# A fused transformer-like layer on one core: three modulation rows moved forward in a hand-written order, and four small edits around the router

## The chip, the cores and the metric

The kernel runs on one core of one Trainium2 chip. The metric is the device time of one execution in microseconds (us), the median of several. The engines are TensorE (PE, matrix products), VectorE (DVE), ScalarE (ACT), GpSimd (POOL) and SyncE (SP, which here only starts transfers). They run side by side, each its own list of instructions in order, and meet at semaphores: an engine stops at a wait until another has counted the semaphore up.

## The reference, cut to what matters

One residual layer for 256 tokens (`S`) of width 2048 (`D`), all in float32:

```
ada = silu(c) @ w_ada + b_ada                  # w_ada: 2048 x (6 x 2048)
sh_m, sc_m, gt_m, sh_f, sc_f, gt_f = split(ada, 6)
h  = rms_norm(x, g_pre_mix) * (1 + sc_m) + sh_m
y  = token_mixer(h)      # h @ w_in; attention heads || gated linear attention; @ w_out
x1 = x + gt_m * rms_norm(y, g_post_mix)
h  = rms_norm(x1, g_pre_ffn) * (1 + sc_f) + sh_f
y  = hier_moe(h)         # top-1 group of 8 experts, top-2 experts inside it, 32 experts in all
x  = x1 + gt_f * rms_norm(y, g_post_ffn)
```

with `rms_norm(x, g) = x * rsqrt(mean(x*x) + 1e-6) * g`. An expert is `(silu(t @ w1) * (t @ w3)) @ w2`, its three matrices 4 MB each.

## The kernel before, in words

**Stages.** The first 230 us build the first two modulation vectors and a first part of the input projection. Then a list called `SCHED`, made by `schedule()` and walked by every engine in the same order, holds the rest of the mixer: 28 slots, each one part of a product with `w_in` on PE (L832; 16 matmul records, some 7 us), and beside it pieces of attention, of the linear attention and of the modulation. After the slots come the output units: products of the mixer's output with `w_out` (two units of two token halves, then the last two quarters of the columns as seven half-size products called `prod` 0 to 6). Then x1, the router, and the experts, one loop pass per tile of 32 token rows.

**Modulation rows.** The four remaining modulation vectors (m = 2 to 5) are matrix-vector products done by DVE: 64 row blocks of `w_ada`, 1 MB each, are loaded by SP and multiplied and added into an accumulator (`accumulate`, L1320 for the first block of a vector, L1322 for the others). They are numbered 1 to 64 here; blocks 33 to 48 are vector 4, blocks 49 to 64 vector 5. The table `ADA_IN` (L78) says how many of them stand in each slot, 28 slots and the four output units; within a slot they stand ahead of the slot's pieces of linear attention. Four buffers hold them, so SP starts the load of a block when the block four earlier has been used (L573 and L574). `loads()` also derives SP's own order from the same table: the blocks are queued in between the loads of the weight units; those of the `w_out` units 8 and 9 (4 MB each, L568) come where the slots 23 and 27 end, four blocks ahead of DVE's use.

**Linear attention at the end of the slots.** PE makes `kv` (L890), DVE turns it into states (L1481, L1483), PE reads them out (`glao`, L900), ACT squares, POOL takes the roots, and DVE multiplies the result by its gate (`gmul`, L1492; (0,0) in slot 26, (1,0) and (0,1) in slot 27, (1,1) behind). Then `glaT` (L910) on PE transposes the first token half; it waits for `gla_sb` to reach 3, that is for three of the four `gmul`, and it stands in PE's list between the last slot product and the first output unit (L923).

**Queues.** SP's transfers and ACT's go through one DMA queue each. ACT starts the row gain `g1b` and the load of unit 10 (L1870) after the second output unit, and half units of 2 MB (L1859, L1872) later.

**Around x1.** For each token half t, ACT squares the quarters of y with a sum (`square_of`), DVE adds the four sums (`total_of`), POOL makes the inverse root in two steps (`rms`: L1976 scale and add, L1979 power), DVE forms x1 (L1510). PE transposes x1 and makes the logits, DVE routes (L1523 to L1576), PE picks the first tile's rows (`pick_rows`, L1014), DVE copies them (L1596), PE transposes them (L1026), DVE scales and shifts (L1599, L1602), and the first expert's products begin (L1064).

**Expert loads.** Five weight buffers of 4 MB. The halves of the first five matrices are started by SP as the `prod` products free their space. All further ones are started as PE passes points of the expert loop, the first of them (L629) behind the first quarter of the first product of expert 0's last tile (`a_half`).

Of the kernel before, what the change touches and what calls it, by code (L numbers as in the profile page):

```python
# [26 lines left out]
D = 2048  # L27
S = 256
P = 128
TT = S // P  # L30
# [10 lines left out]
EPS = 1e-6  # L41
# [10 lines left out]
C_ID, C_LT, C_SUF, C_ONE, C_IOTA, C_NH, C_HALF, C_FOLD, C_FLIP, C_PAIR, C_BKT = 0, 128, 256, 384, 512, 544, 548, 550, 582, 710, 774  # L52
# [22 lines left out]
FILLS = HELD + SLOTS // 2 - 2 * len(BLOCK_UNITS)  # L75
ATT_FROM = 4
MOD_AFTER = {2: 7, 3: 16}
ADA_IN = [1, 1, 1, 1, 1, 1, 1, 1, 2, 2, 2, 2, 0, 3, 3, 3, 2, 2, 2, 1, 1, 3, 3, 2, 2, 2, 2, 1, 4, 4, 4, 4]  # L78
ADA_SLOT = [s for s, n in enumerate(ADA_IN) for _ in range(n)]


# [145 lines left out]
def build(nc, a, out):  # L227
    f32, i32, u32 = mybir.dt.float32, mybir.dt.int32, mybir.dt.uint32
    ALU, ACT, AX = mybir.AluOpType, mybir.ActivationFunctionType, mybir.AxisListType
    SCHED = schedule()  # L230
    ctx = ExitStack()
    with ctx:
# [14 lines left out]
        cst = sb("cst", [P, C_KEEP])  # L247
# [3 lines left out]
        gains = sb("gains", [P, 4, KD])  # L251
        bada = sb("bada", [P, 6, KD])
        mod = sb("mod", [P, 6, KD])
# [3 lines left out]
        st = sb("st", [P, 84])  # L257
# [14 lines left out]
        y, x1T = view(s3, 0, TT, D), view(s4, 0, KD, S)  # L272
# [3 lines left out]
        junk = wk[:, 3584:4096]  # L276
# [21 lines left out]
        xp = wk[:, 2560:3072]  # L298
        wr, wrf = view(wrs, 0, KD, RT_N), wrs
        hit, gated, pick = view(wrf, 0, 2 * TT, ROWS), view(wrf, 128, 2 * TT, ROWS), view(wrf, 256, TT, ROWS)  # L300
# [5 lines left out]
        def rows(t):  # L306

            return resid[:, TT - 1 - t, :].rearrange("p (k q) -> p k q", k=KD)
# [55 lines left out]
        def bank(b, *dims):  # L364
            if not dims:
                return ps[:, b, :]
            return ps[:, b, 0:dims[0] * dims[1]].rearrange("p (n c) -> p n c", n=dims[0])
# [49 lines left out]
        def ada_quarter(n):  # L417
# [36 lines left out]
        g_sb, g_out, x1_row, g_in, xre_in = sem("g_sb"), sem("g_out"), sem("x1_row"), sem("g_in"), sem("xre_in")  # L454
        y_tot, y_sum, y_rs, x1_sb, x1_sq, x1_rs = sem("y_tot"), sem("y_sum"), sem("y_rs"), sem("x1_sb"), sem("x1_sq"), sem("x1_rs")
        x1T_ps, x1T_dve, x1T_act, logT_sb, shs_sb, shs_ps, wr_sb = sem("x1T_ps"), sem("x1T_dve"), sem("x1T_act"), sem("logT_sb"), sem("shs_sb"), sem("shs_ps"), sem("wr_sb")
        pick_sb, pick_c, rows_ps, rows_sb = sem("pick_sb"), sem("pick_c"), sem("rows_ps"), sem("rows_sb")
        gate_c, gated_sb, spread_ps, spread_sb, part_ps, ysum_sb = (
            sem("gate_c"), sem("gated_sb"), sem("spread_ps"), sem("spread_sb"), sem("part_ps"), sem("ysum_sb"))
        log_ps, g_max, e_max, r_exp2, m_sb, rank_ps, route_sb = (  # L460
            sem("log_ps"), sem("g_max"), sem("e_max"), sem("r_exp2"), sem("m_sb"), sem("rank_ps"),
            sem("route_sb"))
# [208 lines left out]
        def _(pe):  # L671
# [3 lines left out]
            for t in range(TT):  # L675
                pe.wait_ge(diag_sb, t + 1)
                for j in range(4):
                    if t and j == 3:
                        pe.wait_ge(xT_sb, 1)
                    for k in range(4):  # L680
                        last = nc.tensor.matmul(bank((4 * t + j) % 7, 4, P)[:, k, :], resid[:, t, P * (4 * j + k):P * (4 * j + k) + P], diag[:, t, :], start=(k == 0), stop=(k == 3))
# [43 lines left out]
            for j in range(len(STAGES)):  # L725
                pe.wait_ge(early_w_in[j % 3], 16 * sum(slab_count(i) for i in range(j % 3, j + 1, 3)))
                for n, u in enumerate(TURN):
# [6 lines left out]
                    last = early_unit(j, u)  # L734
# [9 lines left out]
            for item in SCHED:  # L744
                kind = item[0]
                if kind == "mod":
                    m = item[1]
# [8 lines left out]
                elif kind == "alpha":  # L756

                    if item[1] == 0:
# [3 lines left out]
                        for k in range(KD):  # L762
                            last = nc.tensor.matmul(bank(5)[32 * (k % 4):32 * (k % 4) + 32, 0:S], wzb[:, k, :], hT[:, k, :], start=(k < 4), stop=(k >= KD - 4))
# [114 lines left out]
                elif kind == "kv":  # L878
                    t = item[1]
# [130 lines left out]
            def pick_rows():  # L1010

                for t2 in range(TT):
                    for g in range(4):
                        last = nc.tensor.matmul(bank(0)[32 * g:32 * g + 32, :], pick[:, t2, :], rows(t2)[:, g:KD:4, :], start=(t2 == 0), stop=(t2 == TT - 1))  # L1014
                last.then_inc(rows_ps, 1)
# [12 lines left out]

            pe.wait_ge(x1_row, TT)
            pe.wait_ge(pick_sb, 1)  # L1030
            pick_rows()
            pe.wait_ge(route_sb, 1)
            first_hi = pe.value_load(cums[0:1, 1:2], min_val=1, max_val=MAX_TILES)
            for h in range(2):
# [127 lines left out]
        def _(dve):  # L1162
# [161 lines left out]
            def take_mod(m):  # L1324
                dve.wait_ge(mod_ps, m - 1)
                V.tensor_tensor(mod[:, m, :], mod_bank(m)[:, 16 * m:16 * m + 16], bada[:, m, :], ALU.add).then_inc(mod_sb, 1)
                dve.wait_ge(mod_sb, m - 1)
                if m == 4:
                    V.scalar_tensor_tensor(out=mod[:, m, :], in0=mod[:, m, :], scalar=1.0, in1=gains[:, 2, :], op0=ALU.add, op1=ALU.mult).then_inc(scale_sb, 1)
                    dve.wait_ge(scale_sb, 1)  # L1330
                if m in (2, 5):
                    V.tensor_tensor(mod[:, m, :], mod[:, m, :], gains[:, 1 if m == 2 else 3, :], ALU.mult).then_inc(g_sb, 1)

            def gain_y(u, t):

                if u < 2:
                    dve.wait_ge(proj_sb, FILLS + 2 * u + t + 1)
                else:
                    dve.wait_ge(y_sum, {(2, 0): 5, (3, 0): 6, (3, 1): 7, (2, 1): 8}[u, t])
                dve.wait_ge(g_in, 16)  # L1340
                c = slice(512 * u, 512 * u + 512)
                link(V.tensor_tensor(y[:, t, c], y[:, t, c], g1b[:, c], ALU.mult))

            def total_of(t):
                dve.wait_ge(y_sum, 6 + 2 * t)
                V.tensor_reduce(st[:, 56 + t:57 + t], st[:, 48 + 4 * t:52 + 4 * t], axis=AX.X, op=ALU.add).then_inc(y_tot, 1)

            def sum_of(out_, in0, in1, n, op=ALU.add):

                V.tensor_tensor(out_, in0, in1, op).then_inc(mix_sb, 1)  # L1350
                dve.wait_ge(mix_sb, n)

            def y_at(t, u):
                return y[:, t, 512 * u:512 * u + 512]
# [141 lines left out]
            for t in range(TT):  # L1496
                if t:
                    dve.wait_ge(proj_ps, FILLS + 10)
                    sum_of(y_at(1, 2), y_at(1, 3), bank(4), 13)
                    sum_of(y_at(1, 3), y_at(1, 2), bank(3), 14)  # L1500
                    dve.wait_ge(proj_ps, FILLS + 11)
                    sum_of(y_at(1, 2), y_at(1, 2), bank(1), 15)
                    gain_y(3, 1)
                else:
                    gain_y(2, 0)
                total_of(t)
                gain_y(2 if t else 3, t)
                dve.wait_ge(y_rs, t + 1)
                dve.wait_ge(xre_in, 32)
                V.scalar_tensor_tensor(out=x_again(t), in0=y[:, t, :], scalar=st[:, 58 + t:59 + t], in1=x_again(t), op0=ALU.mult, op1=ALU.add).then_inc(x1_sb, 1)  # L1510
# [81 lines left out]

                return mod[:, m, 8 * h:8 * h + 8].unsqueeze(2).to_broadcast((P, 8, ROWS))

            def copy_rows(h):
                V.tensor_copy(xp[:, S * h:S * h + S], bank(0)[:, S * h:S * h + S]).then_inc(rows_sb, 1)  # L1596

            def scaled(h):
                return V.tensor_tensor(xe[:, 8 * h:8 * h + 8, :], bank(3 + h, 8, ROWS), by_column(4, h), ALU.mult)  # L1599
# [8 lines left out]
            link(V.tensor_copy(gates[:, :, :], R("w")))  # L1608
            dve.nop(nofuse=True).then_inc(route_sb, 1)
            V.memset(spread, 0.0).then_inc(spread_sb, 1)  # L1610
            dve.wait_ge(rows_ps, 1)
            for h in range(2):
                copy_rows(h)
            for h in range(2):
                dve.wait_ge(xe_ps, h + 1)
                scaled(h).then_inc(xe_t, 1)
# [77 lines left out]
        def _(act):  # L1694
# [49 lines left out]
            def squares(t):  # L1744

                act.wait_ge(x1_sb, t + 1)
                A(acc[:, :] if t else resid[:, 1, :], x_again(t), ACT.Square, accum_out=st[:, 60 + t:61 + t]).then_inc(x1_sq, 1)
                act.wait_ge(x1_sq, t + 1)

            def order_rows(t):  # L1750

                if t:
                    act.wait_ge(x1_row, t)
                A(rows(t), x_again(t).rearrange("p (q k) -> p k q", k=KD), ACT.Copy).then_inc(x1_row, 1)
# [123 lines left out]

            def square_of(t, u, mixed_n, n):

                act.wait_ge(y_sum, n - 1)
                act.wait_ge(mix_sb, mixed_n)
                A(junk, y[:, t, 512 * u:512 * u + 512], ACT.Square, accum_out=st[:, 48 + 4 * t + u:49 + 4 * t + u]).then_inc(y_sum, 1)

            square_of(0, 2, 6, 5)
            square_of(0, 3, 12, 6)
            squares(0)
            order_rows(0)
            square_of(1, 3, 14, 7)
            square_of(1, 2, 15, 8)  # L1890

            for t in range(TT):
# [71 lines left out]
        def _(pool):  # L1964
            n_c = [0]

            def link(ins):

                ins.then_inc(pool_c, 1)
                n_c[0] += 1  # L1970
                pool.wait_ge(pool_c, n_c[0])

            def rms(src, dst, width):

                n = src.shape[1]
                nc.gpsimd.tensor_scalar(dst, src, 1.0 / width, EPS, ALU.mult, ALU.add).then_inc(pool_c, 1)  # L1976
                n_c[0] += 1
                pool.wait_ge(pool_c, n_c[0])
                return nc.gpsimd.tensor_tensor(dst, dst, cst[:, C_NH:C_NH + n], ALU.pow)  # L1979
# [53 lines left out]
            pool.memset(ye, 0.0).then_inc(ye_sb, 1)  # L2033
            for t in range(TT):
                pool.wait_ge(y_tot, t + 1)
                rms(st[:, 56 + t:57 + t], st[:, 58 + t:59 + t], D).then_inc(y_rs, 1)
                pool.wait_ge(x1_sq, t + 1)
                rms(st[:, 60 + t:61 + t], st[:, 62 + t:63 + t], D).then_inc(x1_rs, 1)
            pool.wait_ge(g_sb, 2)
            pool.dma_start(gdram[1, :, :], mod[:, 5, :]).then_inc(g_out, 16)  # L2040

            pool.wait_ge(x1_sq, TT)
            pool.memset(ysum[0], 0.0).then_inc(ysum_sb, 1)
            pool.wait_ge(mod_ps, 4)
# [26 lines left out]
```

## Time and profile before

| | us |
|---|---|
| median of 3 runs | 1452.66 |
| lowest, highest | 1451.88, 1452.72 |
| the profiled execution, its own time | 1452.2 |
| span of its profile | 1450.3 |

| engine | busy in the span |
|---|---|
| PE | 84% |
| DVE | 54% |
| ACT | 15% |
| POOL | 4% |

Transfers move 583.52 MB, at 402 GB/s over the span. The chain of waits that ended last is 42% DMA and 33% PE. Such a share is a mean over stages with different limits; what one stage is limited by is read from that stage's rows.

### The profile page before, as it was taken

How to read it: one execution, taken by the hardware profiler on the slowest of the kernel's cores; microseconds unless marked ns; L12 is line 12 of the kernel's file. 1: busy time of each engine (PE TensorE's matmuls, PEld its weight loads, DVE VectorE, ACT ScalarE, POOL GpSimd, SP SyncE). 2: the span in 40 equal slices, each digit the busy share in tenths (PEclk: the TensorE clock that was granted, in tenths of full speed). 3: DMA queues.
4: the chain of work that ended last, by engine and by line, in shares of the span. 5: the costliest groups of instructions: out<-in, count | busy, mean ns of one | idle time of the engine just before them, and what ended most of it. 6: DMA issues, size and time to landing. Idle time of an engine off the chain costs nothing.

```text
span 1450.3 us, 18992 instructions
## 1 busy us (share of the span) xinstructions
PE 1221.5 (84%) x7437; PEld 573.8 (40%) x7438; DVE 780.4 (54%) x1106; ACT 210.4 (15%) x489; POOL 53.6 (4%) x76
## 2 busy tenths in 40 slices
PE   4899999999999989877776667767776679999967
PEld 3678788644444443222232222222222223333322
DVE  5777379897888765433343234323332335555525
ACT  3011131223111041000010001000000001111103
POOL 1000300020000020000000000000000000000020
PEclk9999999999999999888788789888888889999989
DMA  9999977999999899999999999999999999999996
GB/s 354 389 389 377 311 294 293 389 374 382 411 411 405 316 390 423 430 431 431 432 432 433 430 432 431 433 431 432 433 431 431 431 433 433 431 432 431 431 427 263
DMA packets 81653, 583.52 MB, mean 402 GB/s; under 512 B 5376, under 2 KB 30256, under 8 KB 56912
## 3 DMA queue, kind: packets, MB, share of 16 engines
q1 hardware_dynamic: 74256, 564.41, 94.4%
q10 hardware_dynamic: 5808, 14.85, 2.7%
q0 software_dynamic: 1552, 3.75, 0.9%
q8 instruction: 25, 0.41, 0.1%
q14 instruction: 12, 0.10, 0.0%
HBM read 579.30 MB, written 3.69 MB: 402 GB/s over the span
## 4 chain that ended last, share of the span: by engine, by line
DMA 42%; PE 33%; DVE 3%; issue 1%; ACT 1%; POOL 0%; SPq 0%; ACTq 0%; DVEq 0%
DMA stream<-in_w 41%; PE ps L1064 9%; PE ps L832 6%; PE ps L1120 4%; PE ps L1071 3%; PE ps L1020 2%; PE ps L923 2%; PE ps L1014 2%; DVE stream L1350 1%; PE ps L928 1%; PE ps L932 1%; DMA stream<-in_w_out 1%; PE ps L1026 0%; PE ps L890 0%; PE ps L900 0%
## 5 line engine op out<-in xcount | busy, mean ns | idle before, releaser
L1064 PE MATMUL ps<-stream,wk 128*32 128x512 f32 x2304 | 330.0, 711 | 178.8 <-DMA stream<-in_w 178.1
L1589 DVE TENSOR_TENSOR acc<-ps,acc 128x2048 f32<-128x2048 f32 x37 | 84.8, 2291 | 359.2 <-PE ps L1020 359.2
L1064 PEld LDWEIGHTS ps<-stream,wk 128*32 128x32 f32 x2304 | 74.7, 125 | 417.3 <-issue 329.9
L1120 PE MATMUL ps<-stream,cst 128*32 128x512 f32 x1152 | 131.5, 595 | 7.8 <-DMA stream<-in_w 7.8
L717 PE MATMUL ps<-stream 128*128 128x256 f32 x512 | 117.0, 388 | 6.3 <-DVE stream L1196 2.1
L832 PE MATMUL ps<-stream 128*128 128x512 f32 x256 | 112.7, 593 | 0.0
L717 PEld LDWEIGHTS ps<-stream 128*128 128x128 f32 x512 | 99.1, 194 | 26.9 <-issue 7.8
L1071 PEld LDWEIGHTS ps<-cst,wk 128*128 128x128 f32 x576 | 77.3, 209 | 69.7 <-issue 69.7
L1020 PE MATMUL ps<-wk,cst 32*128 32x512 f32 x592 | 92.1, 694 | 0.8 <-ACT wk L1929 0.8
L1210 DVE SCALAR_TENSOR_TENSOR wk<-stream,cc,wk 128x768 f32<-128x768 f32 (+1 forms) x90 | 83.5, 928 | 11.2 <-DMA stream<-in_w_ada 8.6
L1071 PE MATMUL ps<-cst,wk 128*128 128x32 f32 x576 | 85.5, 295 | 0.0
L1589 DVE TENSOR_TENSOR wk<-ps,wk 128x2048 f32<-128x2048 f32 x36 | 82.2, 2282 | 1.6 <-PE ps L1020 1.6
L1322 DVE SCALAR_TENSOR_TENSOR acc<-stream,cc,acc 128x2048 f32<-128x2048 f32 x30 | 70.4, 2348 | 10.0 <-DMA stream<-in_w_ada 8.9
L1637 DVE TENSOR_SCALAR cst<-cst 128x128 f32<-128x128 f32 x36 | 8.2, 228 | 116.3 <-ACT cst L1923 116.3
L1014 PE MATMUL ps<-resid,wrs 128*32 128x512 f32 x592 | 70.2, 592 | 0.2 <-DVE wrs L1576 0.2
L832 PEld LDWEIGHTS ps<-stream 128*128 128x128 f32 x256 | 47.5, 190 | 55.1 <-issue 55.1
L1120 PEld LDWEIGHTS ps<-stream,cst 128*32 128x32 f32 x1152 | 35.9, 109 | 77.7 <-issue 62.2
L1921 ACT ACTIVATE wk<-ps 128x512 f32<-128x512 f32 x36 | 21.5, 597 | 268.8 <-PE ps L1064 268.8
L965 PE MATMUL ps<-stream 128*128 128x512 f32 x112 | 48.6, 594 | 2.0 <-DMA stream<-in_w_out 2.0
L784 PE MATMUL ps<-stream 128*128 128x256 f32 x224 | 49.9, 381 | 0.3 <-PE ps L717 0.3
L1596 DVE COPY wk<-ps 128x256 f32<-128x256 f32 x74 | 27.9, 419 | 36.2 <-PE ps L1014 36.2
L784 PEld LDWEIGHTS ps<-stream 128*128 128x128 f32 x224 | 42.1, 190 | 7.1 <-issue 1.6
(291 smaller groups left out, 1151.9 us busy)
## 6 DMA issues: line engine op xcount, KB each, us to landing
stream<-in_w SPq DMA_DIRECT2D x87, 4096.0 KB, 41.8
stream<-in_w_ada SPq DMA_DIRECT2D x64, 1024.0 KB, 7.7
stream<-in_w SPq DMA_DIRECT2D x16, 2048.0 KB, 11.5
stream<-in_w_in SPq DMA_DIRECT2D x7, 4096.0 KB, 15.5
stream<-in_w_ada SPq DMA_DIRECT2D x64, 384.0 KB, 9.8
stream<-in_w_ada SPq DMA_DIRECT2D x16, 512.0 KB, 9.7
stream<-in_w_in SPq DMA_DIRECT2D x4, 2048.0 KB, 13.4
stream<-in_w_out SPq DMA_DIRECT2D x2, 4096.0 KB, 17.3
```

What stands on the lines that cost most here:

```text
L717: last = nc.tensor.matmul(bank(u if held else HELD, 2, S)[:, part, :], home(k, k + 1)[:, 0, 256 * u + P * part:256 * u + P * part + P], hT ...
L784: last = nc.tensor.matmul(block_bank(b, n), left[:, k, :], right[:, k, :], start=(k == 0), stop=(k == 7))
L832: last = nc.tensor.matmul(bank(fill % 2), hT[:, k, P * half:P * half + P], w[:, k, :], start=(k == 0), stop=(k == KD - 1))
L965: last = nc.tensor.matmul(bank(b), left[:, k, :], right[:, k, :], start=(k == 0), stop=(k == 7))
L1014: last = nc.tensor.matmul(bank(0)[32 * g:32 * g + 32, :], pick[:, t2, :], rows(t2)[:, g:KD:4, :], start=(t2 == 0), stop=(t2 == TT - 1))
L1020: last = nc.tensor.matmul(ps[:, b0 + g, :], spread[32 * g:32 * g + 32, t2, :], ye[32 * g:32 * g + 32, :], start=not onto, stop=True)
L1064: last = nc.tensor.matmul(bank(1 + m)[32 * g:32 * g + 32, :], xe[:, k + g, :], w13[m][:, k + g, :], start=(k == 0), stop=(k == KD - 4))
L1071: last = nc.tensor.matmul(bank(1 + m, 4, ROWS)[:, c, :], ab[m][:, P * c:P * c + P], cst[:, C_FOLD:C_FOLD + ROWS], start=True, stop=True)
L1120: last = nc.tensor.matmul(bank(2)[32 * g:32 * g + 32, :], hid[:, k, :], w2v[:, k, 512 * g:512 * g + 512], start=(k == 0), stop=(k == 3))
L1210: ins = V.scalar_tensor_tensor(out=out_, in0=w, scalar=cc[:, 2, k:k + 1], in1=out_, op0=ALU.mult, op1=ALU.add)
L1322: V.scalar_tensor_tensor(out=acc_m, in0=w, scalar=col, in1=acc_m, op0=ALU.mult, op1=ALU.add).then_inc(ada_done, 1)
L1589: V.tensor_tensor(y4, ps[:, b0:b0 + 4, :], y4, ALU.add).then_inc(ysum_sb, 1)
```

## The change

1. `ADA_IN`: the entries of slots 23 and 24 go from 2 to 3, those of slots 25 and 26 stay 2, slot 27 goes from 1 to 2, and the first three output units get 3 instead of 4. So 51 blocks instead of 48 stand ahead of the output units.
2. x1's root: DVE's `total_of` now adds a sum of three made earlier (`first_three`), the fourth and `D * EPS`, so that POOL takes the power alone. The factor `sqrt(D)` goes into the gain of vector 2. ACT squares quarter 3 of the second half before it orders the first half's rows, and writes the sums in another order.
3. The first picking is done in two halves of 256 columns into two PSUM banks, each with its own semaphore, and each copy waits for its half alone.
4. POOL's clearings of the two expert sums (2048 columns each) wait for `route_sb`, which follows the router's counts.

```diff
-ADA_IN = [1, 1, 1, 1, 1, 1, 1, 1, 2, 2, 2, 2, 0, 3, 3, 3, 2, 2, 2, 1, 1, 3, 3, 2, 2, 2, 2, 1, 4, 4, 4, 4]
+ADA_IN = [1, 1, 1, 1, 1, 1, 1, 1, 2, 2, 2, 2, 0, 3, 3, 3, 2, 2, 2, 1, 1, 3, 3, 3, 3, 2, 2, 2, 3, 3, 3, 4]
...
             pe.wait_ge(pick_sb, 1)
-            pick_rows()
+            for n in range(2):
+                for t2 in range(TT):
+                    for g in range(4):
+                        last = nc.tensor.matmul(bank(5 * n)[32 * g:32 * g + 32, S * n:S * n + S], pick[:, t2, :], rows(t2)[:, g + 8 * n:8 * n + 8:4, :], start=(t2 == 0), stop=(t2 == TT - 1))
+                last.then_inc(rows_ps if n else log_ps, 1)
...
             def total_of(t):
                 dve.wait_ge(y_sum, 6 + 2 * t)
-                V.tensor_reduce(st[:, 56 + t:57 + t], st[:, 48 + 4 * t:52 + 4 * t], axis=AX.X, op=ALU.add).then_inc(y_tot, 1)
+                V.tensor_scalar(st[:, 56 + t:57 + t], st[:, 51 + 4 * t:52 + 4 * t], st[:, 4 + t:5 + t], D * EPS, ALU.add, ALU.add).then_inc(y_tot, 1)
+
+            def first_three(t):
+                dve.wait_ge(y_sum, 5 + 2 * t)
+                link(V.tensor_reduce(st[:, 4 + t:5 + t], st[:, 48 + 4 * t:51 + 4 * t], axis=AX.X, op=ALU.add))
...
                     sum_of(y_at(1, 3), y_at(1, 2), bank(3), 14)
+                    first_three(1)
+                    gain_y(3, 1)
                     dve.wait_ge(proj_ps, FILLS + 11)
                     sum_of(y_at(1, 2), y_at(1, 2), bank(1), 15)
-                    gain_y(3, 1)
                 else:
                     gain_y(2, 0)
+                    first_three(0)
                 total_of(t)
...
-            dve.wait_ge(rows_ps, 1)
             for h in range(2):
-                copy_rows(h)
+                dve.wait_ge(*((rows_ps, 1) if h else (log_ps, 3)))
+                copy_rows(h, 5 * h)
...
             squares(0)
+            square_of(1, 3, 14, 7)
             order_rows(0)
-            square_of(1, 3, 14, 7)
             square_of(1, 2, 15, 8)
...
                 pool.wait_ge(y_tot, t + 1)
-                rms(st[:, 56 + t:57 + t], st[:, 58 + t:59 + t], D).then_inc(y_rs, 1)
+                nc.gpsimd.tensor_tensor(st[:, 58 + t:59 + t], st[:, 56 + t:57 + t], cst[:, C_NH:C_NH + 1], ALU.pow).then_inc(y_rs, 1)
...
+            pool.wait_ge(route_sb, 1)
             pool.wait_ge(x1_sq, TT)
             pool.memset(ysum[0], 0.0).then_inc(ysum_sb, 1)
             pool.wait_ge(mod_ps, 4)
             pool.memset(ysum[1], 0.0).then_inc(ysum_sb, 1)
-            pool.wait_ge(route_sb, 1)
```

DVE's list from slot 21 to the first output unit, before. `acc` and `wk` are the accumulators of vectors 4 and 5, `resid` holds the states, `stream` behind L1492 the gated result:

```order
L1322 SCALAR_TENSOR_TENSOR acc<-stream,cc,acc 128x2048 x8
L1481 COPY resid<-ps 128x256 x4
L1483 SCALAR_TENSOR_TENSOR resid<-resid,st,ps 128x256 x4
L1322 SCALAR_TENSOR_TENSOR acc<-stream,cc,acc 128x2048 x2
L1483 SCALAR_TENSOR_TENSOR resid<-resid,st,ps 128x256 x8
L1322 SCALAR_TENSOR_TENSOR acc<-stream,cc,acc 128x2048 x4
L1492 SCALAR_TENSOR_TENSOR stream<-ps,st,stream 128x256 x2
L1322 SCALAR_TENSOR_TENSOR acc<-stream,cc,acc 128x2048
L1492 SCALAR_TENSOR_TENSOR stream<-ps,st,stream 128x256 x6
L1320 TENSOR_SCALAR wk<-stream,cc 128x2048
L1322 SCALAR_TENSOR_TENSOR wk<-stream,cc,wk 128x2048 x3
```

The same piece of DVE's list now (its line numbers are those of the changed file: L1326 is the old L1322, L1324 the old L1320, L1500 the old L1492):

```order
L1326 SCALAR_TENSOR_TENSOR acc<-stream,cc,acc 128x2048 x9
L1489 COPY resid<-ps 128x256 x4
L1491 SCALAR_TENSOR_TENSOR resid<-resid,st,ps 128x256 x4
L1326 SCALAR_TENSOR_TENSOR acc<-stream,cc,acc 128x2048 x3
L1491 SCALAR_TENSOR_TENSOR resid<-resid,st,ps 128x256 x8
L1326 SCALAR_TENSOR_TENSOR acc<-stream,cc,acc 128x2048 x3
L1324 TENSOR_SCALAR wk<-stream,cc 128x2048
L1500 SCALAR_TENSOR_TENSOR stream<-ps,st,stream 128x256 x2
L1326 SCALAR_TENSOR_TENSOR wk<-stream,cc,wk 128x2048 x2
L1500 SCALAR_TENSOR_TENSOR stream<-ps,st,stream 128x256 x6
L1326 SCALAR_TENSOR_TENSOR wk<-stream,cc,wk 128x2048 x3
```

One more block now stands ahead of the first states, two ahead of the last states, and three ahead of the six gate multiplications at the end, of which the first four are those that `glaT` waits for.

SP's list around the two loads of `w_out` units, before:

```order
L565 DMA stream<-in_w_in 128x16x512
L574 DMA stream<-in_w_ada 128x2048 x9
L568 DMA stream<-in_w_out 128x16x512
L574 DMA stream<-in_w_ada 128x2048 x7
L568 DMA stream<-in_w_out 128x16x512
L574 DMA stream<-in_w_ada 128x2048 x12
```

and now:

```order
L565 DMA stream<-in_w_in 128x16x512
L574 DMA stream<-in_w_ada 128x2048 x10
L568 DMA stream<-in_w_out 128x16x512
L574 DMA stream<-in_w_ada 128x2048 x9
L568 DMA stream<-in_w_out 128x16x512
L574 DMA stream<-in_w_ada 128x2048 x9
```

One block is queued ahead of unit 8 that stood behind it, and three ahead of unit 9.

## Rows read from the trace of the kernel before

**Rows 1.** Windows: us, busy of each engine, TensorE clock, DMA share, GB/s.

```profile
core 0: us, PE busy (x) PEld busy (x) DVE busy (x) ACT busy (x) POOL busy (x), PEclk, DMA share, GB/s
600.00:1400.00 800.00, 624.55 (x4732) 221.24 (x4728) 317.16 (x565) 77.58 (x158) 0.00 (x0) 0.88 1.00 432
...
540.00:544.00 4.00, 3.75 (x36) 1.15 (x40) 2.41 (x9) 0.04 (x1) 0.00 (x0) 1.00 0.54 164
```

**Rows 2.** Timeline of PE: start, us, line, shapes, count [idle before it, ended by].

```profile
381.58 1.95 PE L900 MATMUL ps<-resid,stream 128*64 128x256 f32 x16
...
394.33 14.00 PE L832 MATMUL ps<-stream 128*128 128x512 f32 x32
408.37 1.09 PE L910 MATMUL ps<-cst,stream 128*128 128x128 f32 x8
...
467.84 34.60 PE L965 MATMUL ps<-stream 128*128 128x512 f32 x80 [2.03 <-DMA stream<-in_w_out]
```

**Rows 3.** Timeline of DVE, slot 21 to the output units.

```profile
358.12 19.56 DVE L1322 SCALAR_TENSOR_TENSOR acc<-stream,cc,acc 128x2048 f32<-128x2048 f32 x8
377.60 1.41 DVE L1481 COPY resid<-ps 128x256 f32<-128x256 f32 x4
379.04 1.66 DVE L1483 SCALAR_TENSOR_TENSOR resid<-resid,st,ps 128x256 f32<-128x256 f32 x4
...
385.50 3.35 DVE L1483 SCALAR_TENSOR_TENSOR resid<-resid,st,ps 128x256 f32<-128x256 f32 x8
...
398.87 4.83 DVE L1322 SCALAR_TENSOR_TENSOR acc<-stream,cc,acc 128x2048 f32<-128x2048 f32 x2 [5.30 <-DMA stream<-in_w_ada]
...
406.67 1.65 DVE L1492 SCALAR_TENSOR_TENSOR stream<-ps,st,stream 128x256 f32<-128x256 f32 x4
...
427.17 4.80 DVE L1322 SCALAR_TENSOR_TENSOR wk<-stream,cc,wk 128x2048 f32<-128x2048 f32 x2 [2.79 <-DMA stream<-in_w_ada]
```

**Rows 4.** Windows, as Rows 1: two stretches before the output units.

```profile
378.00:398.87 20.87, 20.87 (x84) 10.02 (x83) 15.20 (x21) 3.52 (x17) 2.88 (x5) 1.00 1.03 404
398.87:411.30 12.43, 12.39 (x36) 5.73 (x35) 11.45 (x13) 2.17 (x5) 0.00 (x0) 1.00 1.02 422
```

**Rows 5.** The DMA issue at 408.36: timeline, then issues (KB, us to landing).

```profile
408.36 0.38 SPq L568 DMA_DIRECT2D stream<-in_w_out  x1
...
stream<-in_w_out SPq DMA_DIRECT2D x1, 4096.0 KB, 16.2
```

**Rows 6.** Idle PE and the clock behind it: timeline, then windows as Rows 1.

```profile
594.96 5.34 PE L1064 MATMUL ps<-stream,wk 128*32 128x512 f32 x32 [2.62 <-DMA stream<-in_w]
605.12 2.71 PE L1064 MATMUL ps<-stream,wk 128*32 128x512 f32 x16 [3.75 <-DMA stream<-in_w]
...
596.00:600.00 4.00, 4.00 (x28) 0.87 (x17) 0.00 (x0) 0.00 (x0) 0.00 (x0) 0.59 0.98 422
604.00:612.00 8.00, 6.88 (x36) 2.92 (x40) 1.71 (x4) 0.28 (x1) 0.00 (x0) 0.63 1.01 434
```

**Rows 7.** Timeline around the second half's root: DVE and POOL.

```profile
518.39 0.69 DVE L1342 TENSOR_TENSOR stream<-stream,acc 128x512 f32<-128x512 f32 x1
...
513.14 0.19 POOL L1976 TENSOR_SCALAR st<-st 128x1 f32<-128x1 f32 x1 [4.57 <-ACT resid L1747]
...
518.53 0.60 POOL L1976 TENSOR_SCALAR st<-st 128x1 f32<-128x1 f32 x1 [4.56 <-DVE st L1346]
519.21 0.54 POOL L1979 TENSOR_TENSOR st<-st,cst 128x1 f32<-128x1 f32 x1
```

**Rows 8.** Timeline of DVE in the router, beside POOL's second clearing.

```profile
529.21 0.49 DVE L1531 TENSOR_SCALAR wk<-wk 128x2 f32<-128x2 f32 x1
```

**Rows 9.** Timeline of PE: a logit product, then the first picking and transposing.

```profile
518.81 2.03 PE L985 MATMUL ps<-stream,wrs 128*64 128x128 f32 x32 [0.44 <-ACT stream L1895]
...
536.29 1.92 PE L1014 MATMUL ps<-resid,wrs 128*32 128x512 f32 x16 [0.24 <-DVE wrs L1576]
538.75 0.77 PE L1026 MATMUL ps<-cst,wk 128*128 128x128 f32 x4 [0.54 <-DVE wk L1596]
```

More of the change, by code:

```diff
@@ L1331, in take_mod @@
                 if m in (2, 5):
-                    V.tensor_tensor(mod[:, m, :], mod[:, m, :], gains[:, 1 if m == 2 else 3, :], ALU.mult).then_inc(g_sb, 1)
+                    V.scalar_tensor_tensor(out=mod[:, m, :], in0=mod[:, m, :], scalar=math.sqrt(D) if m == 2 else 1.0, in1=gains[:, 1 if m == 2 else 3, :], op0=ALU.mult, op1=ALU.mult).then_inc(g_sb, 1)
             def gain_y(u, t):
@@ L1593, in by_column, with copy_rows @@
                 return mod[:, m, 8 * h:8 * h + 8].unsqueeze(2).to_broadcast((P, 8, ROWS))
-            def copy_rows(h):
-                V.tensor_copy(xp[:, S * h:S * h + S], bank(0)[:, S * h:S * h + S]).then_inc(rows_sb, 1)
+            def copy_rows(h, b=0):
+                V.tensor_copy(xp[:, S * h:S * h + S], bank(b)[:, S * h:S * h + S]).then_inc(rows_sb, 1)
             def scaled(h):
@@ L1879, in square_of @@
             def square_of(t, u, mixed_n, n):
+                at = 48 + 4 * t + (5 - u if t else u)
                 act.wait_ge(y_sum, n - 1)
                 act.wait_ge(mix_sb, mixed_n)
-                A(junk, y[:, t, 512 * u:512 * u + 512], ACT.Square, accum_out=st[:, 48 + 4 * t + u:49 + 4 * t + u]).then_inc(y_sum, 1)
+                A(junk, y[:, t, 512 * u:512 * u + 512], ACT.Square, accum_out=st[:, at:at + 1]).then_inc(y_sum, 1)
             square_of(0, 2, 6, 5)
```

## The prediction

> **What bounds the kernel now.** I read the windows first. From 600 to 1400 us the DMA share is 1.00 at 432 GB/s [rows 1]: the experts' stage is bound by its 4 MB weight loads, and none of the edits changes its bytes. What can change the time is when that stage starts, because it is shifted as a whole. Its first further load is issued at PE's first expert product, and there the DMA queue runs dry for a moment: share 0.54 in 540 to 544, about 4 x 0.46 = 1.8 us idle [rows 1]. The loads before that one are issued as the seven `prod` products end (SP's waits in the code), so they follow PE too. So I then read PE's timeline backwards from the products. It is an unbroken row of matmuls from 381.58 to the end of the second output unit: the slot products end at 408.33, `glaT` starts at 408.37, and the only idle time until the `prod` run is 2.03 us at 467.84, for unit 10's load [rows 2]. Third, DVE's timeline beside it, for who holds PE where: the four gate multiplications that `glaT` needs end at 406.67 + 1.65 = 408.32 [rows 3], the very moment PE gets there. Here is no slack at all. Fourth, why DVE is not earlier: at 398.87 it had stood idle for 5.30 us on a modulation block [rows 3], and the DMA shares around that are 1.03 and 1.02 [rows 4]. In this stretch the transfers set the pace of the blocks, and the blocks set DVE's.
>
> **Term A, the moved blocks at `glaT`: +7.0.** The change puts block 49, 50 and 51 ahead of the four multiplications, where 48 stood last. DVE's list in the section on the change shows it. When can block 51 be there? Block 46 lands at 398.87, where DVE starts [rows 3]. A block is 1.049 MB, at 422 GB/s [rows 4] one per 2.49 us, so block 51 lands at 398.87 + 5 x 2.49 = 411.3. The cadence can be checked further on: block 52 at 413.8, then unit 9 (issued at 408.36, landed 16.2 later [rows 5], at 424.6), then block 53 at 424.6 + 2.5 = 427.1, and DVE takes it up at 427.17 after waiting [rows 3]. The change cannot bring block 51 earlier: up to it the queue carries the same bytes, it only swaps block 46 with unit 8, and there was no idle DMA time to fill. SP's issue is not late either: a load waits for the block four earlier, number 47, done at about 403.8 also in the new order. So DVE starts block 51 at 411.3, ends it 4.83 / 2 = 2.4 later at 413.7, and the four multiplications, 1.65, end at 415.3. PE starts `glaT` at 415.35 instead of 408.37: +7.0.
> On the way there DVE also reaches the first states one block later. They ended at 379.04 + 1.66 = 380.70; the run of eight blocks takes 19.56, one costs 2.45 [rows 3], so now 383.15, and PE, which wants them at 381.58 [rows 2], waits 1.6. The second states, with two blocks more (ended 385.50 + 3.35 = 388.85, now 393.7), are in time for PE, which reads them out last before 394.33, so from 392.4 then and from 394.0 now. The 1.6 is not added: PE then arrives at `glaT` at 409.9, still 5.4 before its data.
> Bounds: if blocks came as fast as DVE eats them, three more cost 7.3 and the 5.30 of idle time swallows most: +2.0. If they come at the 404 GB/s of the window before [rows 4], +7.6. I take 7.0, since the landings at 398.87 and 427.17 both fit it.
>
> **Term B, the clock behind that wait: +2.3.** PE now idles for 5.4 us in one piece at about 410 to 415. After idle times of 2.62 and 3.75 us the granted clock is 0.59 in 596 to 600 and 0.63 in 604 to 612 [rows 6], a mix of 0.5 (1.2 GHz) and 1.0 (2.4 GHz). The half-speed share is 0.82 of 4 us and 0.74 of 8 us, so 3.3 and 5.9 us at half speed, which cost half of that: 1.6 and 3.0. The products behind `glaT` are dense and nothing hides their length, so I take the middle, 2.3. Bounds: 0, as the 2.03 of idle time at 467.84 [rows 2] may have left the clock alone, and 3.0.
> The Trainium skill, "TensorE: Matmul & The Clock Gate", section "HAM oscillation — how this bites in real kernels", says that a TensorE left idle falls back to the half rate and pays once more in slow matmuls after each such gap. That speaks against this change. By it the sum keeps term B; without it the sum is 2.3 lower. The rows of idle time in this trace agree, with 0.59 and 0.63.
>
> **Term C, the wait for unit 10: -2.0.** PE's output units now run some 9.3 us later (A + B). Unit 10 is issued behind the second one, so its issue moves from 438.6 to about 448. But its bytes don't add to the queue: left then are the row gain (1.05 MB), unit 10 (4.19) and about three blocks (3.15), 8.4 MB, at about 405 GB/s 20.7 us, landing at about 471. PE asks for it at 465.8 + 9.3 = 475.1. So the 2.03 of waiting [rows 2] vanish, and the `prod` run starts 7.3 later than before. What is late next? The half unit loaded after the second unit is asked for three products (20.8 us) later, so it has room. DVE is held for vector 4 until PE's fold behind that second unit, now at about 447, and then has one block less than before up to the differences for the later products, so it keeps its distance to PE. Bounds: 0 if the queue runs dry for longer and unit 10 stays the last to come, -2.03 otherwise.
> In the blocks' place behind the output units three DVE steps of 2.4 are gone; they stood in front of a wait of DVE on the half unit's load, off the path, and I count them at nothing.
>
> **Term D, the small edits: -1.0.** They lie behind the products, on the path to the first expert product, and there the DMA queue idles for 1.8, so all of a gain below 1.8 counts.
> Root in one step: L1976 took 0.60 and its successor began 0.68 after it [rows 7]. But the same step took 0.19 when DVE was quiet (513.14), and here it ended at 519.13, just behind DVE's multiplication at 518.39 + 0.69 = 519.08 [rows 7]. The power would meet the same multiplication, so only 0.19 + 0.08 goes: -0.3, with -0.68 as the other end.
> The Trainium skill, "SBUF — State Buffer", section "SBUF: two separate sides", has DVE and GpSimd share a port pair that the loser waits for whole, for DVE operations with two SBUF inputs only against a GpSimd operation that reads SBUF. By this rule the saving is 0.3, without it 0.68. The 0.60 against 0.19 in the trace agrees.
> The three-quarter sum and the fourth's moved square lie in DVE's and ACT's idle time before the last product ends: 0. ACT's row ordering starts later by one square but the three steps end together.
> Clearings: the TENSOR_SCALAR on two elements at 529.21 took 0.49 [rows 8] against 0.16 to 0.19 for such small steps elsewhere, -0.3. Moved, they run from about 536 to 540 beside copies out of PSUM, and the first user, PE's first addition, comes at 543.8: 0, or +0.5 if they hold up a DVE step.
> First picking in halves: PE's picking is 1.92, then a copy, then the transposing starts 0.54 after [rows 9]. Now the first copy lies beside the second half, and 0.5 goes. The picking has 32 records instead of 16; L985 does 32 with 128 columns in 2.03 [rows 9], so +0.1 at least if the loads of the small operand set the pace: together -0.4. The other end is the 3.1 that 32 records would take at the pace of L1026 (0.77 for the 8 of its 4 matmuls): 3.1 - 1.92 - 0.5 = +0.7.
> 0.3 + 0.3 + 0.4 = 1.0, between -1.5 and +0.6.
>
> **Sum.** 7.0 + 2.3 - 2.0 - 1.0 = +6.3. Against the profiled execution's own 1452.2 (a span of 1450.3 and 1.9 around it, which the change leaves alone) this is 1458.5; the median of the runs is 0.5 above that execution, and I forecast for the median: 1459.0.
>
> **Rivals.**
> *It gets faster as the three blocks free unit 10's load.* Fewer bytes after 439, unit 10 lands sooner, PE's 2.03 go, and D comes on top: -3.0, 1449.7. For it: the one idle time of PE in [rows 2] is that load. Against it: the queue was full from 378 on [rows 4], so a block moved forward moves something else back, and bytes landed by 467.8 stay the same. It decides as soon as block 51 could be used before 404.3, since then DVE needs 2.4 + 1.65 and is at `glaT`'s time; that is 7 us ahead of its landing. 0.07.
> *The wait is as long but the clock holds.* 7.0 - 2.0 - 1.0 = +4.0, 1456.7. For it: the wait lies between two dense stretches, those of [rows 6] between thinner ones. 0.2.
> *The blocks arrive faster than I say, DVE's own time decides.* +2.0 and no clock loss, 2.0 - 2.0 - 1.0 = -1.0, 1451.7, within 0.2%. For it only that the landings inside the run are computed, not seen. 0.06.
> *The queue runs dry as well.* With DVE waiting for PE's fold, SP has no free buffer, and ACT issues unit 10 late: the transfers idle for about 3 us at 447, unit 10 and the half units land that much later, PE waits again, and 2 to 3 come on top: 1461.5. Against it: by term C unit 10 has 4 us of room, with such a gap still 1. 0.1.
>
> **How the numbers follow.** The forecast itself has 0.57; its own range is 1457 to 1460.5, by term B's and term D's likelier ends. About 0.2% is what a measurement of this kernel can tell from no change, 2.9 us. Slower: 0.57 + 0.2 + 0.1 = 0.87. Same: 0.06. Faster: 0.07. The range has to take in the clock rival (1456.7) and the dry queue (1461.5), and ends half way towards the case within 0.2% below: 1454.8 to 1461.8, which leaves out less than 2 in 10.
>
> **What would show it.** In PE's timeline after: one idle time of 5 to 5.5 us before `glaT` (L910), ended by DVE's L1500, and one of 1.6 before the first `glao` (L900) at 381.6, ended by L1491. DVE idle on a block at about 396 to 401 and again by tenths before each of the next four. A granted clock below 1.00 in the window behind 415. No wait before the `prod` run, which starts 7 us later, at about 475. POOL's power alone before x1. A prediction that is wrong shows `glaT` at 408 to 410; or the late `prod` run is there but the first expert load is not later; or a wait for unit 10 that is still there.

## The result, and the profile after

| | us |
|---|---|
| before, median of 6 runs | 1452.64 (1451.88 to 1453.39) |
| changed, median of 6 runs | 1458.18 (1456.32 to 1459.80) |
| ratio changed to before, 95% interval | 1.0036 (1.0024 to 1.0048) |
| changed, profiled execution and its span | 1457.18, 1455.3 |

The change made the kernel slower by 5.5 us (the interval of the ratio reaches from 3.5 to 7.0), where 6.3 were forecast. One of the twelve executions of the later kernel e6 took 1982.13 us at a mean granted clock of 0.556, where all others of this document stand at 0.92 to 0.93, and is left out. PE's timeline of the changed kernel (start, us, line, shapes, count, idle time before it and what ended it) answers to [rows 2]:

```profile
382.88 1.95 PE L900 MATMUL ps<-resid,stream 128*64 128x256 f32 x16 [1.56 <-DVE resid L1491]
...
395.62 14.00 PE L832 MATMUL ps<-stream 128*128 128x512 f32 x32
414.94 1.97 PE L910 MATMUL ps<-cst,stream 128*128 128x128 f32 x8 [5.32 <-DVE stream L1500]
416.70 15.10 PE L923 MATMUL ps<-stream 128*128 128x512 f32 x32
...
474.24 6.25 PE L965 MATMUL ps<-stream 128*128 128x512 f32 x14
```

The unbroken row of matmuls now has a hole of 5.32 us before `glaT`, ended by the gate multiplication L1500. `glaT` takes 1.97 where it took 1.09, and the unit behind it 15.10 instead of the 13.90 that the other units take. The `prod` run starts at 474.24, not 467.84, and has no wait for unit 10 before it any more. DVE's timeline beside it answers to [rows 3]:

```profile
357.79 22.02 DVE L1326 SCALAR_TENSOR_TENSOR acc<-stream,cc,acc 128x2048 f32<-128x2048 f32 x9
...
401.01 4.84 DVE L1326 SCALAR_TENSOR_TENSOR acc<-stream,cc,acc 128x2048 f32<-128x2048 f32 x2 [5.49 <-DMA stream<-in_w_ada]
405.98 1.29 DVE L1324 TENSOR_SCALAR wk<-stream,cc 128x2048 f32<-128x2048 f32 x1
407.18 0.87 DVE L1500 SCALAR_TENSOR_TENSOR stream<-ps,st,stream 128x256 f32<-128x256 f32 x2
408.48 4.84 DVE L1326 SCALAR_TENSOR_TENSOR wk<-stream,cc,wk 128x2048 f32<-128x2048 f32 x2 [0.42 <-DMA stream<-in_w_ada]
413.23 2.44 DVE L1500 SCALAR_TENSOR_TENSOR stream<-ps,st,stream 128x256 f32<-128x256 f32 x6
```

DVE again stands idle for more than 5 us on a block (now number 47 at 401.01). Behind it come the next four blocks and the first multiplication, and DVE reaches the other multiplications at 413.23. Of these 12.2 us it works 4.84 + 1.29 + 0.87 + 4.84 = 11.8 and waits only 0.4: behind block 47 the landings and DVE's own work keep nearly the same pace. The clock is seen in the window of the changed kernel (columns as in [rows 1]):

```profile
412.00:420.00 8.00, 5.06 (x13) 3.16 (x14) 7.90 (x9) 1.68 (x4) 0.00 (x0) 0.57 1.01 414
444.00:450.00 6.00, 6.00 (x22) 2.54 (x21) 3.23 (x6) 1.28 (x3) 0.00 (x0) 1.00 0.43 135
```

0.57 means that most of the eight microseconds were granted 1.2 GHz. The second row shows the transfers running dry around ACT's issue of unit 10 at 447.60: a share of 0.43 in 6 us, so 3.4 us idle. DVE had stood idle for 7.50 us until PE's fold (the small product L687 that sums vector 4), and in that time it freed no buffer for SP's next block, so SP issued none between 439.20 and 452.36:

```profile
446.67 0.17 DVE L1330 TENSOR_TENSOR mod<-ps,bada 128x16 f32<-128x16 f32 x1 [7.50 <-PE ps L687]
```

Behind the products the small edits do what they say. POOL's power, alone, then DVE's small step in the router (which answers to [rows 8]), then PE's first picking (to [rows 9]):

```profile
525.31 0.92 POOL L2047 TENSOR_TENSOR st<-st,cst 128x1 f32<-128x1 f32 x1 [5.20 <-DVE st L1350]
```

```profile
535.31 0.17 DVE L1541 TENSOR_SCALAR wk<-wk 128x2 f32<-128x2 f32 x1
```

```profile
542.14 1.93 PE L1034 MATMUL ps<-resid,wrs 128*32 128x256 f32 x32 [0.24 <-DVE wrs L1586]
544.00 0.44 PE L1026 MATMUL ps<-cst,wk 128*128 128x128 f32 x2
...
545.50 3.64 PE L1068 MATMUL ps<-stream,wk 128*32 128x512 f32 x32 [0.46 <-DVE wk L1612]
```

The root takes 0.92 where the two steps took 519.21 + 0.54 - 518.53 = 1.22 [rows 7]: 0.30 saved. The TENSOR_SCALAR takes 0.17 instead of 0.49. The first expert product starts at 545.50; before, it was at 540.25.

The account of the profiled executions: `glaT` +6.57 (in this execution PE is about 0.3 earlier up to there than before, so +6.9 on equal footing), the `prod` run +6.40, the first expert product +5.25, the span +5.0 (1455.3 against 1450.3).

### The profile page after: what moved, and what is told of

The parts are those of the page before. It is cut to its first block, busy times and chain, and to the rows that moved or that the text cites. A ratio compares the mean times of both kernels' runs of the same rounds, so it can differ in the third digit from the quotient of the medians.

```text
span 1455.3 us, 19027 instructions
## 1 busy us (share of the span) xinstructions
PE 1221.5 (84%) x7453; PEld 575.7 (40%) x7454; DVE 780.4 (54%) x1108; ACT 210.3 (14%) x489; POOL 53.0 (4%) x74
## 4 chain that ended last, share of the span: by engine, by line
DMA 39%; PE 36%; DVE 3%; issue 1%; ACT 0%; POOL 0%; SPq 0%; ACTq 0%; DVEq 0%
DMA stream<-in_w 37%; PE ps L1068 10%; PE ps L1124 5%; PE ps L965 3%; PE ps L832 3%; PE ps L1075 3%; PE ps L1020 3%; PE ps L1014 2%; PE ps L923 2%; DVE acc L1326 2%; DMA stream<-in_w_ada 2%; PE ps L928 1%; PE ps L932 1%; PE ps L1026 1%; PE ps L1110 0%
## 5 line engine op out<-in xcount | busy, mean ns | idle before, releaser
L1326 DVE SCALAR_TENSOR_TENSOR acc<-stream,cc,acc 128x2048 f32<-128x2048 f32 x30 | 70.4, 2348 | 10.0 <-DMA stream<-in_w_ada 8.8
## 6 DMA issues: line engine op xcount, KB each, us to landing
stream<-in_w SPq DMA_DIRECT2D x16, 2048.0 KB, 11.8
```

The lines of the kernel that those rows point to most:

```text
L1326: V.scalar_tensor_tensor(out=acc_m, in0=w, scalar=col, in1=acc_m, op0=ALU.mult, op1=ALU.add).then_inc(ada_done, 1)
```

## The experiments

Each but e7 was timed beside the kernel before, whose median was 1453.30 beside e1 to e4, 1453.63 beside e5, e6 and e8, and 1452.89 beside e9. Ratios are to the kernel before; where two experiments are compared across these groups, the ratios count more than the medians.

**e1: the small edits without the table.**

```diff
-ADA_IN = [..., 3, 3, 3, 3, 2, 2, 2, 3, 3, 3, 4]
+ADA_IN = [..., 3, 3, 2, 2, 2, 2, 1, 4, 4, 4, 4]
```

> The changed kernel with the old ADA_IN: only the root step, the picking in halves and the moved clearings are left. My theory (all the loss is in the moved blocks, the small edits gain 1.0): glaT at 408.4, the wait of 2.0 for unit 10 back, first expert product 1.1 earlier than before (about 539.2), time 1451.6, that is -1.0 against before. Rival (the small edits cost, or are given back by the DMA queue, since it is full behind them): time 1452.6 or above, although the first expert product is earlier.

Measured: 1452.32, ratio 0.9989 (0.9980 to 0.9998). In its profile `glaT` is at 408.27, the wait for unit 10 is back at 2.0, and the first expert product starts at 538.94, 1.3 before the old one. So the small edits gain about 1 us up to the experts; the interval of the ratio reaches from 0.3 to 2.9 us of gain.

**e2: the table alone**, on the kernel before.

> The kernel before with the new ADA_IN alone. My theory: glaT waits 5.3 for DVE and starts at about 415, the clock is at half for a stretch behind it (2.1 more), no wait for unit 10, the prod run starts 6.5 to 7 later, and nothing is gained behind it: time +6.5, about 1459.1. Rival (the small edits share in the loss): less than +5.5, since the changed kernel as a whole is +5.5.

Measured: 1459.82, ratio 1.0042 (1.0028 to 1.0055). The loss is the table's. But its 6 us or so are made up a little differently:

```profile
382.87 3.31 PE L900 MATMUL ps<-resid,stream 128*64 128x256 f32 x16 [2.12 <-DVE resid L1483]
...
414.48 1.97 PE L910 MATMUL ps<-cst,stream 128*128 128x128 f32 x8 [3.22 <-DVE stream L1492]
416.24 14.49 PE L923 MATMUL ps<-stream 128*128 128x512 f32 x32
```

Here the small wait before the first states' reading (L900) is 2.12 and already costs clock: the product takes 3.31, not 1.95, and the next slot's products begin 1.6 later for it. PE then arrives later at `glaT` and waits only 3.22 there. `glaT` starts at 414.48 all the same: the start is set by DVE, wherever PE spends its time before.

**e3: the gate multiplications ahead of the blocks**, on the changed kernel. SP's order is unchanged, with 51 blocks ahead of unit 9.

```diff
-    beside[26] += [("gsq", 1), ("gmul", 0, 0)]
-    beside[27] += [("gmul", 1, 0), ("gmul", 0, 1), ("glaT", 0)]
+    beside[26] = [("gmul", 0, 0)] + beside[26] + [("gsq", 1)]
+    beside[27] = [("gmul", 1, 0), ("gmul", 0, 1)] + beside[27] + [("glaT", 0)]
```

> The changed kernel with all its blocks where SP has them (51 ahead of unit 9's load), but in DVE's list the gate multiplication (0,0) stands at the head of slot 26 and (1,0), (0,1) at the head of slot 27, ahead of the blocks. My theory (the loss is DVE's order, not the moved bytes): multiplications done by about 409.3, glaT at 409.6 to 409.9 (only the 1.6 at the first glao is left), no clock loss, unit 9 still lands in time at about 432, PE waits 0.5 for unit 10 as the queue's bytes by then are the same, time 1451.6 to 1452. Rival (the three blocks ahead of unit 9 cost by themselves, as PE waits for unit 9 or for the queue): still 1456 or more, with a wait of PE on in_w_out at L928 or L965. A second rival (moving blocks forward frees unit 10): unit 10 lands 3 blocks earlier, no wait, 1450 or less.

Measured: 1450.87, ratio 0.9985 (0.9976 to 0.9994). PE's timeline of this kernel:

```profile
382.39 1.95 PE L900 MATMUL ps<-resid,stream 128*64 128x256 f32 x16 [1.55 <-DVE resid L1491]
...
408.97 1.04 PE L910 MATMUL ps<-cst,stream 128*128 128x128 f32 x8
409.85 13.90 PE L923 MATMUL ps<-stream 128*128 128x512 f32 x32
...
467.00 3.27 PE L965 MATMUL ps<-stream 128*128 128x512 f32 x7 [0.64 <-DMA stream<-in_w_out]
```

and DVE's, with the four multiplications done at 407.19 + 1.65 = 408.84:

```profile
407.19 1.65 DVE L1500 SCALAR_TENSOR_TENSOR stream<-ps,st,stream 128x256 f32<-128x256 f32 x4
408.76 4.80 DVE L1326 SCALAR_TENSOR_TENSOR wk<-stream,cc,wk 128x2048 f32<-128x2048 f32 x2
```

No wait at `glaT`, full clock, and the whole loss is gone, with the same three blocks ahead of unit 9's load. So the loss is DVE's order, not the moved bytes. The same run refutes the thought that a move forward frees unit 10's load: PE comes to the `prod` run 0.6 later than before and unit 10 lands at 467.0, where it landed at 467.8 before [rows 2] and at 467.6 in e1. Three blocks moved forward freed at most 0.8 us of it, where three blocks' transfers are some 7 us. Where those 0.6 to 0.8 come from was not tried.

**e4: PE kept busy in the wait**, on the changed kernel.

```diff
+                    if t == 0:
+                        for _ in range(5):
+                            nc.tensor.matmul(bank(7), ident, hT[:, 0:2, :], start=True, stop=True)
                     pe.wait_ge(gla_sb, 3 + t)
```

> The changed kernel; PE does five 128x512 products of the identity (into a bank nobody reads) ahead of its wait for the gate multiplications, 4.6 us of the 5.3 it idles. My theory (the half clock behind glaT comes from that idle time, and costs 2.1): clock 1.00 through 412 to 420, glaT 1.1 and the unit behind it 13.9 long instead of 1.97 and 15.10, time 2 less than the changed kernel, about 1456.1, and its runs closer together. Rival (the slow matmuls behind the wait have another cause, such as the transfers): glaT and L923 stay at 1.97 and 15.1, time as the changed kernel, 1458.2.

Measured: 1455.89, ratio 1.0020 (1.0011 to 1.0029).

```profile
409.40 4.46 PE L907 MATMUL ps<-stream,cst 128*128 128x512 f32 x10
415.07 1.09 PE L913 MATMUL ps<-cst,stream 128*128 128x128 f32 x8 [1.22 <-DVE stream L1503]
416.00 13.90 PE L926 MATMUL ps<-stream 128*128 128x512 f32 x32
```

`glaT` starts no earlier (415.07), but it and the unit behind it have their full-speed lengths, 1.09 and 13.90, and the `prod` run starts 1.9 earlier than in the changed kernel. So about 2 us of the loss were the clock: 2.0 from `glaT` to the end of that unit in the traces, 2.3 by the ratios. This is the second, separate price of an idle TensorE. The page "TensorE: Matmul & The Clock Gate" of the Trainium skill, section "HAM oscillation — how this bites in real kernels", names this price; the trace agrees, with 1.97 and 15.10 against 1.09 and 13.90.

**e5: 50 blocks ahead instead of 51.**

```diff
-ADA_IN = [..., 3, 3, 3, 3, 2, 2, 2, 3, 3, 3, 4]
+ADA_IN = [..., 3, 3, 3, 3, 2, 2, 1, 4, 3, 3, 4]
```

> The changed kernel with 50 blocks ahead of the output units (one in slot 27, not two). My theory (glaT waits for the landing of the last block ahead of the multiplications, one per 2.49): block 50 lands at 408.5, the multiplications end at about 412.6, PE idles 3.0 at glaT, which starts 2.4 earlier than in the changed kernel; the clock falls all the same or for one stretch less; the wait for unit 10 is away; time about 1455.8, 2.4 less than the changed kernel. Rival (the cost is a fixed one of having vector 5's blocks ahead of the multiplications, or sits in the units' loads): within 0.7 of the changed kernel.

Measured: 1454.12, ratio 1.0007 (0.9998 to 1.0015), by the ratios 4.2 below the changed kernel, not 2.4. The mechanism holds, the size was off:

```profile
383.24 3.06 PE L900 MATMUL ps<-resid,stream 128*64 128x256 f32 x16 [2.15 <-DVE resid L1491]
...
412.37 1.09 PE L910 MATMUL ps<-cst,stream 128*128 128x128 f32 x8 [0.74 <-DVE stream L1500]
```

`glaT` starts at 412.37, 2.57 before the changed kernel's, one block's landing as expected. But PE was itself late in this execution, by the clock behind L900, and waited only 0.74. So no clock was lost behind `glaT`, and in this execution that is the rest: the `prod` run starts 4.6 earlier (469.64), 2.6 by the block and 2.0 by the clock. The clock lost behind L900 cost nothing, as PE would have waited at `glaT` instead. Whether the other executions were alike is not shown; their times lie between 1452.1 and 1456.0.

**e6: the last two blocks' loads held back until unit 10 has landed**, on e1.

```diff
                         sp.wait_ge(ada_done, i - 3)
+                    if i >= 62:
+                        sp.wait_ge(unit_in[0], unit_landed(10))
```

> The old table with the small edits (as e1), and SP holds the last two blocks' loads until unit 10 has landed. My theory (unit 10 waits for bytes ahead of it in the transfers, so it comes sooner only if bytes are put behind it): unit 10 lands 2.1 MB or about 5 sooner, the 2.0 of PE's idle time before the prod run vanish, the prod run starts at about 465.8. But DVE's chain from the half unit's landing at 478.6 and ACT's row ordering then set x1, so only 0.3 to 0.6 of the 2.0 arrive at the end: 0.5 less than e1. Rival (the queue's order does not matter, the wait is ACT's late issue): the wait of 2.0 is still there. Second rival: PE is all that counts, 2.0 less than e1.

Measured: 1450.43 (the median without the execution named under the result), ratio 0.9984 (0.9976 to 0.9993). PE's wait is gone:

```profile
465.48 0.31 PE L942 MATMUL ps<-wk,cst 128*128 128x40 f32 x2
465.62 16.55 PE L967 MATMUL ps<-stream 128*128 128x512 f32 x38
```

Unit 10 landed at 462.8 instead of 467.6. That is how unit 10 comes sooner: bytes put behind it. But at the first expert product only 0.24 of the 2.05 is left (538.70 against 538.94 in e1), as expected from ACT's list: the square that x1 needs starts at 517.05, right behind the row ordering.

```profile
513.39 3.75 ACT L1766 ACTIVATE resid<-resid 128x2048 f32<-128x2048 f32 x1
517.05 0.61 ACT L1896 ACTIVATE wk<-stream 128x512 f32<-128x512 f32 x1
```

Its median lies 1.9 below e1's although the trace gives 0.24 up to the first expert product. The intervals of the two overlap. Of the 2.4 between the spans of the two profiles (1448.8 and 1451.2), 2.2 arise behind the last landing, by the clock (e9 and the last section).

**e8: e6, and ACT orders the first half's rows after the copies of the transposes.**

```diff
-            order_rows(0)
             square_of(1, 2, 15, 8)
...
                 if t == 0:
+                    order_rows(0)
                     squares(1)
```

> e6, and ACT orders the first half's rows (3.7) only after it has squared the last quarter and copied the first half's transposes. My theory: x1's second half no longer waits for ACT, and the 2.0 that PE gained before the prod run reach the first expert product: 2.0 less than e1, about 3 less than before, 1449.6. Rival (DVE's chain from the half unit holds x1 all the same): as e6.

Measured: 1450.26, ratio 0.9980 (0.9971 to 0.9988). The second half's transposes start at 519.87, 2.3 before e1's 522.17, but the first expert product at 537.32, 1.6 before e1's. 0.46 of the difference is visible: PE now waits for ACT's last copy, which stands behind the row ordering. So of the 2.0 forecast 1.6 arrive. The medians of e8 and e6 lie only 0.2 apart though the traces differ by 1.4 at the first expert product; e8's profile lost 2.2 at its end (see e9).

**e7: the first picking whole again**, on the changed kernel; a single execution.

> The changed kernel with the first picking whole again. My theory: between the first picking and the first expert product the distance goes back from 3.36 to 3.96, and the picking itself takes 1.92 as in halves (1.93); the rest of the trace as in the changed kernel. Rival (the clearings beside the copies hold DVE up and it is they that make the difference): the distance stays at 3.4 or is more than 4.0, as POOL now clears beside these copies.

```profile
543.39 1.92 PE L1014 MATMUL ps<-resid,wrs 128*32 128x512 f32 x16 [0.25 <-DVE wrs L1582]
545.86 0.77 PE L1026 MATMUL ps<-cst,wk 128*128 128x128 f32 x4 [0.54 <-DVE wk L1602]
547.36 3.64 PE L1064 MATMUL ps<-stream,wk 128*32 128x512 f32 x32 [0.73 <-DVE wk L1608]
```

From picking to first product 3.97, in halves 3.36: the halves save 0.61. 32 short records take 1.93, 16 long ones 1.92, so the shorter form costs nothing. The clearings now run beside these copies, and the copies take what they took (0.76 for two, 0.42 for one of the halves). Its one time, 1462.66, is not compared: its `glaT` starts 0.5 later than the changed kernel's, the unit behind it takes 15.86, and PE's clock is at 0.50 in 1425 to 1430 and 0.51 in 1430 to 1435.

**e9: e8, with one product in PE's wait for the last quarter of w2, an expert's third matrix.**

```diff
                         if k == 3 and final:
+                            nc.tensor.matmul(bank(1), ident, rows(0)[:, 0:4, :], start=True, stop=True)
                             pe.wait_ge(unit_in[1], 16 * 8)
```

> e8, and in the last expert PE does one 128x512 product of the identity (0.9 us, into a bank that is free) where it waits 1.42 for the last quarter of w2. The ends of the profiles differ though their waits are the same: from the last landing in the first half of the last w2 to the end of the span it is 23.9 where the clock stayed at 1.00 and 25.3 to 26.2 where it was at half for a stretch (the profiles of e8 and of the old table among them). My theory (that stretch hangs on PE's short idle times between w2's quarters): with the wait filled the end is 23.9 again, time 0 to 2 less than e8, 1449.3, runs closer together. Rival (the remaining waits of 0.19 and 0.81 or the time before do it alike, or the filler only delays): the same as e8, 1450.3, or slower.

Measured: 1449.61, ratio 0.9974 (0.9965 to 0.9984): the lowest ratio of all, 3 to 4 us below the kernel before. The middle half of its runs lies within 0.5 us, that of e8's within 1.0. PE's timeline at the end, of e8 and then of e9:

```profile
1429.30 1.06 PE L1126 MATMUL ps<-stream,cst 128*32 128x512 f32 x8 [1.40 <-DMA stream<-in_w]
1431.17 1.80 PE L1022 MATMUL ps<-wk,cst 32*128 32x512 f32 x8 [0.81 <-ACT wk L1942]
1432.91 4.69 PE L1144 MATMUL ps<-wk,cst 128*128 128x512 f32 x8
```

```profile
1426.89 1.12 PE L1124 MATMUL ps<-resid,cst 128*128 128x512 f32 x2
1428.38 1.06 PE L1127 MATMUL ps<-stream,cst 128*32 128x512 f32 x8 [0.36 <-DMA stream<-in_w]
1430.25 1.14 PE L1022 MATMUL ps<-wk,cst 32*128 32x512 f32 x8 [0.81 <-ACT wk L1943]
1431.32 3.70 PE L1145 MATMUL ps<-wk,cst 128*128 128x512 f32 x8
```

The additions behind the last product take 1.80 and 4.69 in e8's profile and 1.14 and 3.70 in e9's. One profile of e9 cannot prove that the stretch is gone for good, since the kernel before and e6 showed the fast end without the filler. The closer runs speak for it, but they were taken beside another group of runs, whose kernel before was itself 0.74 faster than e8's: against its own kernel before, e9's median gains 3.3 and e8's 3.4. So a gain of e9 over e8 is not shown.

## Why the prediction was right

**What bounds.** The tie at `glaT` was the right place. In the six kernels with 48 blocks ahead, or with the multiplications first, it starts at 407.7 to 409.0; with 50 at 412.4; with 51 at 414.5 to 415.4, whatever PE did before.

**Term A, +7.0.** The wait was 5.32, forecast 5.4; the multiplications were wanted at 415.3 and the start was 414.94. The landing of block 47 carried it, at 401.01 where the forecast's cadence has 398.87 + 2.49 = 401.4. From there to 413.23 DVE's own work fills 11.8 of 12.2 us, so the later landings added at most 0.4. The alternative end of +2.0 (blocks as fast as DVE eats them) is out by DVE's wait of 5.49, which did not shrink. e3 shows that the term is order alone.

**Term B, +2.3.** 0.88 on `glaT` and 1.20 on the unit, 2.1 (2.0 by the starts, as the records overlap); by e4's ratio 2.3. In e2 it was 1.4 behind `glaT` and 1.6 already behind the first states, where PE's wait at `glaT` swallows it. In e7 it was 2.8 behind `glaT` (1.97 and 15.86). So the mechanism is shown, but the size differs between executions, and that the middle of 1.6 and 3.0 met this one so closely is partly luck.

**Term C, -2.0.** The wait is gone. Unit 10 landed at 471.8, 2.4 us before the `prod` run began at 474.24. That the forecast says 471 is luck: its own terms give 448 + 20.7 = 468.7. From its issue at 447.60 the load took 24.2, with 382 GB/s over that time, so 9.2 MB went by instead of 8.4. The dry spell that a rival priced at about 3 us was there, 3.4 us idle in 444 to 450; what did not follow is the wait, as unit 10 still had room.

**Term D, -1.0.** From the end of the `prod` run to the first expert product it took 23.68 before and 22.56 now: -1.1. By parts: root 0.30 (forecast 0.3), router 0.3 (forecast 0.3), picking 0.6 (forecast 0.4). Only the picking was also tried alone (e7). That the power, 0.92 here against 0.54 before, waits for DVE's multiplication is read from the order of the rows and was not tried.

**The sum.** +6.3 was forecast; +5.25 at the first expert product and +5.5 in the medians came out. By the starts in the two traces A is +6.9, B +2.0, C -2.2 and D -1.1, and PE was 0.3 earlier up to the slots in this execution. So the miss of 1.05 is made up of small ones: 0.3 by that earlier start, 0.1 in A, 0.3 in B, 0.2 in C and 0.1 in D. They all lie on the same side, and 6.3 is inside the interval of the measured loss, 3.5 to 7.0.

**The rivals.** The gain by a freed unit 10 is refuted by e3. The clock that holds needed help (e4). The dry queue was there, as long as its rival said, and cost nothing at the `prod` run.

## What to carry to other kernels

Before moving work forward on an engine, write down when its data lands: behind a full queue a step moved forward becomes a wait, and everything behind it in that engine's list waits too. To make one load come sooner, put bytes behind it (e6, 4.8 us sooner), not other bytes further ahead (e3, at most 0.8), and ask what the next wait is: of e6's 2.05 only 0.24 reached the first expert product. And count an idle TensorE twice, for the wait and for the slow matmuls that can follow it; cheap filler products took the second part away in e4 (in e9 this is only likely).

## What the runs showed of the hardware that I had not expected

- The end of this kernel differs by 2.3 us between profiles with nearly the same waits. From the start of the products on the last quarter of w2 to the end of the span it is 18.9 to 19.0 us in the kernel before, the changed one, e4, e5, e6 and e9, 20.3 to 20.4 in e2 and e3, and 21.2 in e1 and e8. In the longer ones PE's clock falls for a stretch there: 0.66 in 1430 to 1435 in e8, 1.00 in e6. This alone makes a single run of this kernel uncertain by 2 us.
- The same idle time does not always cost clock: 2.12 and 2.15 before L900 did in e2 and e5 (3.31 and 3.06 for 1.95), 2.21 in e7 and 1.56 in the changed kernel did not.
